# Order of the first pair's nine products in the up projection of a fused two-layer encoder kernel

## The reference, cut to what matters

```python
def conv_ffn(x, g, w_up, conv_w, conv_b, w_down, conv_buf):
    up = rmsnorm(x, g) @ w_up                      # (T, 1024) @ (1024, 2 * 2816)
    full = jnp.concatenate([conv_buf, up], axis=1)
    c = conv_b + full[:, 0:T] * conv_w[0]
    for j in range(1, CONV_W):
        c = c + full[:, j:j + T] * conv_w[j]
    y = (gelu(c[..., :D_FF]) * c[..., D_FF:]) @ w_down
```

## Time and profile before

| | |
|---|---|
| median of 3 runs | 2530.64 us |
| the profiled execution, its own time | 2534.01 us |
| its span | 2532.2 us (1.8 us lie around it) |
| TensorE busy | 2455.9 us, 97% of the span |
| VectorE, ScalarE, GpSimd busy | 1655.4, 1052.1, 579.3 us |
| TensorE in the chain that ended last | 85% of the span |
| mean granted TensorE clock | 0.986 of full speed |

### The profile page before, as it was taken

One profiled execution on the slowest core, in us unless ns is written; L12 is line 12 of the kernel. 1 busy time (PEld: TensorE's weight loads), 2 busy tenths in 40 slices (PEclk: granted clock), 3 DMA queues, 4 the chain that ended last, 5 costly groups with the idle time before them and its releaser, 6 DMA issues.

```text
span 2532.2 us, 41744 instructions
## 1 busy us (share of the span) xinstructions
PE 2455.9 (97%) x16499; PEld 2384.9 (94%) x16499; DVE 1655.4 (65%) x2825; ACT 1052.1 (42%) x1905; POOL 579.3 (23%) x526
## 2 busy tenths in 40 slices
PE   8999989889999999999999999998999999999998
PEld 8999878889999999999999998887999999999997
DVE  3116789788888887464611267888888888864554
ACT  6324544443333333343433355444433333333443
POOL 0001234542222221010110113337322222200111
PEclk9999999999999999999999999998999999999999
DMA  4442322212222223555525333211222222245554
GB/s 149 131 131 93 110 80 65 63 49 70 77 77 74 64 76 110 190 170 162 192 70 154 108 112 104 69 48 53 69 76 77 77 68 70 77 157 175 180 166 157
DMA packets 234903, 265.88 MB, mean 105 GB/s; under 512 B 15287, under 2 KB 207573, under 8 KB 232533
## 3 DMA queue, kind: packets, MB, share of 16 engines
q1 hardware_dynamic: 234708, 263.21, 32.8%
HBM read 213.06 MB, written 50.11 MB: 104 GB/s over the span
## 4 chain that ended last, share of the span: by engine, by line
PE 85%; DVE 8%; issue 3%; POOL 2%; ACT 1%; DMA 1%; SPq 0%; DVEq 0%; POOLq 0%; ACTq 0%
PE bank L317 26%; PE bank L319 25%; PE bank L318 25%; PE bank L1041 2%; DVE prob L1936 1%; PE bank L968 1%; DVE hc L1997 1%; PE bank L1026 1%; PE bank L1010 1%; PE bank L1051 0%; DVE mixA L1964 0%; PE bank L990 0%; PE bank L921 0%; POOL wN L1682 0%; PE bank L1020 0%
## 5 line engine op out<-in xcount | busy, mean ns | idle before, releaser
L317 PE MATMUL bank<-actH,wb 128*128 128x384 f32 (+1 forms) x1552 | 509.6, 328 | 0.3
L318 PE MATMUL bank<-actL,wb 128*128 128x384 f32 (+1 forms) x1552 | 505.4, 326 | 0.0
L319 PE MATMUL bank<-actH,wb 128*128 128x384 f32 (+1 forms) x1552 | 504.7, 325 | 0.0
L317 PE MATMUL bank<-wzH,actH 128*128 128x256 f32 (+3 forms) x1296 | 370.1, 286 | 5.0 <-DVE wzL L1811 4.1
L319 PE MATMUL bank<-wzH,actL 128*128 128x256 f32 (+3 forms) x1296 | 365.3, 282 | 0.0
L318 PE MATMUL bank<-wzL,actH 128*128 128x256 f32 (+3 forms) x1296 | 364.9, 282 | 0.0
L317 PEld LDWEIGHTS bank<-actH,wb 128*128 128x128 f32 x1552 | 292.8, 189 | 5.5 <-issue 4.7
L318 PEld LDWEIGHTS bank<-actL,wb 128*128 128x128 f32 x1552 | 293.4, 189 | 0.5
L319 PEld LDWEIGHTS bank<-actH,wb 128*128 128x128 f32 x1552 | 293.6, 189 | 0.0
L317 PEld LDWEIGHTS bank<-wzH,actH 128*128 128x128 f32 (+1 forms) x1296 | 237.4, 183 | 7.6 <-issue 5.9
L317 PE MATMUL bank<-tH,wb 128*128 128x384 f32 x704 | 237.3, 337 | 1.2 <-ACT vn L1632 1.2
(11 more groups left out here) (289 smaller groups left out, 5229.4 us busy)
## 6 DMA issues: line engine op xcount, KB each, us to landing
raw<-in_w_up SPq DMA_DIRECT2D x88, 512.0 KB, 4.6
raw<-in_w_down SPq DMA_DIRECT2D x88, 512.0 KB, 3.6
g_scratch<-cv SPq DMA_DIRECT2D x44, 545.0 KB, 3.2
rawz<-in_w_in SPq DMA_DIRECT2D x22, 1024.0 KB, 5.5
zb<-z_scratch SPq DMA_DIRECT2D x16, 1156.0 KB, 5.4
tHf<-g_scratch SPq DMA_DIRECT2D x88, 192.0 KB, 3.6
z_scratch<-zst SPq DMA_DIRECT2D x128, 128.0 KB, 1.8
raw<-in_w_out SPq DMA_DIRECT2D x128, 128.0 KB, 2.9
```

The lines of the kernel that those rows point to most:

```text
L317: pe.matmul(out, aH, bH, start=first, stop=False)
L318: pe.matmul(out, aH, bL, start=False, stop=False)
L319: return pe.matmul(out, aL, bH, start=False, stop=last)
```

## The change

Three engines get another order, for the first pair of each layer alone. The work is the same.

TensorE: P1, P2, E, F, P5, `norm_sum`, P6, P7, `norm_row`, P3, P4. The waits before E and F move with them, and P2 gets the wait for `b_l` (low parts) of count 8.

ScalarE: `square_last(5)`, `(6)` and `(7)` follow each other, then come the `norm_high` of the last chunk with `first_copy(0)` between them, then all four `sum_high`, then all four `sums_high`. Before, the `sum_high` and `sums_high` stood between the squares and the `norm_high`.

VectorE: the last three `add_out`, with `weights_low(0, 1)` between them, then all eight `norm_low`, then the low parts of the sums (`tL` 0, three `sum_low`, `tL` 1, `tL` 2). Before, the latter came first and between. From `take` 1 on the order is the old one; the counts waited for follow the new numbering (`product_at`).

GpSimd: the order is kept. The weight sums of the second pair wait for P5, P6, P7 and P3 of the first by their new numbers.

```diff
--- before.py
+++ after.py
@@ -473,6 +473,11 @@
 
             return (l * (NF + NF + NF // 2) + p + 1) * 16
 
+        def product_at(p, name):
+
+            return (("P1", "P2", "E", "F", "P5", "P6", "P7", "P3", "P4") if p == 0 else
+                    ("P1", "P5", "P2", "P6", "P7", "E", "P3", "P4", "F")).index(name) + 1
+
         def step_mm(l, i, m=KT - 1):
 
             c, f = i // NF, i % NF
@@ -1132,37 +1137,54 @@
                         else:
                             pe.wait_ge(take_r, 9 * q - 9 + count)
 
+                    def plain_gate():
+                        if first:
+                            pe.wait_ge(act_l, act_at(n, 2) + KT)
+                        free(6, 24)
+                        plain(4, t[:, 0], t[:, 1])
+
+                    def plain_value():
+                        pe.wait_ge(w_l, weight_at(l, p, 1))
+                        free(9, 24)
+                        plain(5, t[:, 2], t[:, 3])
+
                     pe.wait_ge(w_l, weight_at(l, p, 0))
                     low_parts(4)
                     free(1, 21)
                     quarter(0, t[:, 0, LO], t[:, 1, LO], actH[:, LO, C0], actL[:, LO, C0])
 
+                    if first:
+                        low_parts(8)
+                        free(2, 22)
+                        quarter(1, t[:, 0, HI], t[:, 1, HI], actH[:, HI, C0], actL[:, HI, C0])
+                        plain_gate()
+                        plain_value()
+
                     pe.wait_ge(s_l, 4 * q + 1)
                     low_parts(12)
                     free(7, 23)
                     quarter(2, Sx[:, 0, 0], Sx[:, 0, 1], tH[:, 0], tL[:, 0])
 
-                    free(2, 22)
-                    quarter(1, t[:, 0, HI], t[:, 1, HI], actH[:, HI, C0], actL[:, HI, C0])
+                    if first:
+                        pe.wait_ge(x_r, l * N_X + 16)
+                        norm_sum(pe, n, 2)
+                    else:
+                        free(2, 22)
+                        quarter(1, t[:, 0, HI], t[:, 1, HI], actH[:, HI, C0], actL[:, HI, C0])
 
                     pe.wait_ge(s_l, 4 * q + 3)
                     low_parts(16)
                     pe.wait_ge(copy_r, q + 1)
                     quarter(0, Sx[:, 1, 0], Sx[:, 1, 1], tH[:, 1], tL[:, 1])
-                    if first:
-                        pe.wait_ge(x_r, l * N_X + 16)
-                        norm_sum(pe, n, 2)
 
                     low_parts(20)
                     free(8, 24)
                     quarter(3, Sx[:, 2, 0], Sx[:, 2, 1], tH[:, 2], tL[:, 2])
 
                     if first:
-                        pe.wait_ge(act_l, act_at(n, 2) + KT)
-                    free(6, 24)
-                    plain(4, t[:, 0], t[:, 1])
-                    if first:
                         norm_row(pe, n, 2)
+                    else:
+                        plain_gate()
 
                     pe.wait_ge(s_l, 4 * q + 4)
                     low_parts(24)
@@ -1175,8 +1197,7 @@
                     quarter(3, t[:, 2, HI], t[:, 3, HI], actH[:, LO, C1], actL[:, LO, C1])
 
                     if not first:
-                        pe.wait_ge(take_r, 9 * q)
-                    plain(5, t[:, 2], t[:, 3])
+                        plain_value()
 
                 for p in range(NF):
                     pair(p)
@@ -1577,24 +1598,19 @@
                 for k in range(4):
                     act.wait_ge(t_r, l * 12 + k + 1)
                     act.activation(tH[:, 0, k], xw[:, 4 + k], ACT.Copy).then_inc(b_h, 1)
-                for s in range(3):
-                    sum_high(0, s)
                 square_last(5)
-                sum_high(0, 3)
-                sums_high(0)
                 square_last(6)
-                sums_high(1)
                 square_last(7)
                 act.wait_ge(bank_free, F0 + WU + KT)
                 norm_high(act, n, 2, 0)
                 norm_high(act, n, 2, 1)
                 first_copy(0)
-                sums_high(2)
-                norm_high(act, n, 2, 2)
-                norm_high(act, n, 2, 3)
-                sums_high(3)
-                for m in range(4, KT):
+                for m in range(2, KT):
                     norm_high(act, n, 2, m)
+                for s in range(4):
+                    sum_high(0, s)
+                for k in range(4):
+                    sums_high(k)
 
                 for p in range(NF):
                     ahead = p + 1 < NF
@@ -1753,7 +1769,7 @@
                         pool.wait_ge(raw_in[0], raw_at(l, p))
                         pool.wait_ge(raw_in[1], raw_at(l, p))
                     if p:
-                        pool.wait_ge(mm, tile_mm(l, p - 1, (2, 4, 5, 7)[s]))
+                        pool.wait_ge(mm, tile_mm(l, p - 1, product_at(p - 1, ("P5", "P6", "P7", "P3")[s])))
                     else:
                         pool.wait_ge(mm, l * MMS + WU + (5, 5, 6, 6)[s])
                     if s in (1, 3):
@@ -2103,37 +2119,29 @@
                 for k in range(4):
                     part_low(actL[:, 4 + k, C0], xw[:, k], actH[:, 4 + k, C0], 4 + k + 1)
                 add_out(4)
+                add_out(5)
+                weights_low(0, 1)
+                add_out(6)
+                add_out(7)
+                dve.memset(upb1[:, 0:PAD], 0.0).then_inc(x_r, 1)
+                dve.memset(upb2[:, 0:PAD], 0.0).then_inc(x_r, 1)
+                for m in range(KT):
+                    norm_low(dve, n, 2, m)
                 for k in range(4):
                     part_low(tL[:, 0, k], xw[:, 4 + k], tH[:, 0, k], 16 + k + 1)
                 sum_low(0, 0)
-                add_out(5)
-                weights_low(0, 1)
                 sum_low(0, 2)
-                add_out(6)
                 sum_low(0, 1)
-                add_out(7)
-                dve.memset(upb1[:, 0:PAD], 0.0).then_inc(x_r, 1)
-                dve.memset(upb2[:, 0:PAD], 0.0).then_inc(x_r, 1)
-
-                def second_low(k):
+                for k in range(4):
                     dve.wait_ge(t_r, l * 12 + 4 + 2 * k + 2)
                     part_low(tL[:, 1, k], tLf[:, 1, k], tH[:, 1, k], 20 + 2 * k + 1)
-
-                second_low(0)
-                second_low(1)
-                norm_low(dve, n, 2, 0)
-                norm_low(dve, n, 2, 1)
-                second_low(2)
-                second_low(3)
                 for k in range(4):
                     part_low(tL[:, 2, k], tLf[:, 2, k], tH[:, 2, k], 12 + k + 1)
-                for m in range(2, KT):
-                    norm_low(dve, n, 2, m)
 
                 def take(p, i, out, b, other):
 
                     q = l * NF + p
-                    dve.wait_ge(mm, tile_mm(l, p, TAKEN[i]))
+                    dve.wait_ge(mm, tile_mm(l, p, product_at(p, TAKEN[i])))
                     dve.tensor_tensor(out, bank[b][:, 0:out.shape[1]], other, ALU.mult if i in (6, 9) else ALU.add).then_inc(take_r, 1)
 
                 U0, U1, U2 = slice(PAD, PAD + 384), slice(PAD + 384, PAD + 768), slice(PAD + 768, PAD + TC)
@@ -2308,7 +2316,7 @@
 INIT = 10
 
 
-TAKEN = {1: 4, 2: 3, 3: 2, 4: 5, 5: 5, 6: 6, 7: 7, 8: 8, 9: 9}
+TAKEN = {1: "P6", 2: "P2", 3: "P5", 4: "P7", 5: "P7", 6: "E", 7: "P3", 8: "P4", 9: "F"}
 
 
 _INS = ["x_prompt", "x_sample", "cache_k", "cache_v", "state_C", "state_n", "state_m", "cache_conv", "attn_norm",
```

## The result

The changed kernel takes 2553.5 us in place of 2530.0: the ratio is 1.0094, 95% interval 1.0081 to 1.0107. It is **slower by 23.6 us**. The forecast was 2549.6, in a range of 2540 to 2559.

A forecast was written before the change was run, and what follows sets the result against it. TensorE, busy for 97% of the span, was taken as the bound, so its idle and slow time count. The first take 8.3 us later per layer plus one clock fall, 2 x 8.3 + 2.4 = 19.0, on 2530.6 gives 2549.6; range 2540 to 2559.

The forecast's parts named there:

- The gate of E: TensorE's start of E, waiting for all eight `norm_low`: forecast at 511.7, between 509.3 and 514.3, after idling 13.1 us.
- E and F at half clock: E and F restart at half clock after the wait: 7.1 + 2.4 = 9.5 us, to 521.2.
- The first take: VectorE's first take behind P6: forecast at 526.7 in place of 518.42, 8.3 us later.
- From the first take to the second pair's P6: Stretch behind P6 of the first pair, set by VectorE's chain: forecast unchanged at 24.95 us, P6 at 551.7.
- The clock at the second pair: TensorE's 3.6 us wait before the second pair's P6: clock falls in one of the two layers, 2.4 us.
- Behind P6 VectorE's chain has the same links: From the first take to the second pair's P6: the chain starts 8.3 us late and keeps its length, 24.95 us.
- the rival on the tail: The 24.95 us behind P6 are waits for E and F, so TensorE sets the pace: 2523.4 us; chance 0.03.
- `norm_sum` one product earlier: TensorE issues `norm_sum` before P6: claimed to give nothing, as `norm_mean` stands behind take 1, which waits for P6.
- The full lock: VectorE's `norm_low` and GpSimd take strict turns of 1.5 us: E at 514.1, 2554.4 us in all; chance 0.15.
- The 0.9 us per `norm_low`: Price of each VectorE `norm_low` while GpSimd works, from 1.81 us for two; 0.48 without.

The follow-up runs named there:

- squares_late: The changed kernel with ScalarE's squares 6 and 7 moved behind `norm_high` and `sum_high`: ratio 1.0020, +5.1 us against the kernel before.
- mean_first: The changed kernel with `norm_mean` alone moved ahead of take 1 on VectorE: ratio 1.0064, +16.2 us against the kernel before.
- before_diag_early: The kernel before, with `norm_sum` ahead of P6, `norm_mean` ahead of the last six `norm_low`, `norm_diag` right behind take 3: ratio 0.9993, -1.8 us.

## Why the prediction was right

*The gate of E.* Right. Forecast 511.7, measured 511.61, and from P1, which came 0.7 us earlier in that run, 18.1 in place of 17.6. Its reasons hold one by one: add 5 ended at 503.4 for 504.0, square 7 ran at 503.45 for 504.1, the `norm_high` ended at 507.9 for 508.8, and the eight `norm_low` took 7.15 for 6.6. squares_late shows the cause. That the two starts of E agree to 0.1 us is partly luck: P1 came 0.7 us early, and the `norm_low` took 0.6 longer than I had them.

*E and F at half clock.* 9.76 and 9.2 us for 9.5. P5 found its parts ready, as forecast.

*The first take* came 8.9 and 8.6 us later than before when both are counted from P1 (33.1 for 24.3 in the first layer), for 8.3. P5, `norm_sum` and P6 took what was said.

*From the first take to the second pair's P6:* 25.4 for 24.95, another 0.5 us. In the trace VectorE's `sum_low(1, 3)` takes 1.75 us beside a sum of GpSimd, where it took 0.69 before.

*The clock at the second pair* is **the term that was mis-sized**. I counted one fall of 2.4 us in the two layers. It fell in both, in waits of 4.7 and 3.6 us, and cost 2.8 and 2.4, 5.2 in all. This is 2.8 of the 4.6 us by which the forecast fell short. The other 1.8 us are the P6 of the second pair, 9.4 and 9.1 us later, counted from P1, for 8.3.

*"Behind P6 VectorE's chain has the same links"* held as a sum, and **its reason did not hold**. I took 24.95 us as VectorE's own work with GpSimd's power of 3.12 us in it, and in the rival on the tail I asked only for waits for E and F. mean_first shows 3 us in it that are neither: the power of 0.86 us lasts 3.12 beside VectorE's reads, and `norm_diag` is stretched by GpSimd's sums. I said that `norm_sum` one product earlier gives nothing as long as `norm_mean` stands behind take 1. That was right, and moving `norm_mean` was worth 6.5 us in the tail of the two layers.

*The full lock* as a rival: E would have come at 514.1, and it came at 511.6. But the turns that it describes are there, and **what I held against it was misread**. The 0.9 us per `norm_low` is a mean of 0.59 and 1.30: the first of the two started late in an instruction of GpSimd, the second beside a whole one.

```profile
507.85 0.59 DVE L432 SCALAR_TENSOR_TENSOR actL<-xT,gains,actH 128x322 fp32r<-128x322 f32 x1 [0.64 <-ACT actH L426]
...
508.36 1.30 DVE L432 SCALAR_TENSOR_TENSOR actL<-xT,gains,actH 128x322 fp32r<-128x322 f32 x1
```

In the changed kernel five `norm_low` pass while GpSimd makes five instructions (the last four are shown), and the other three, behind it, take 0.47 each:

```profile
505.34 1.12 POOL L365 TENSOR_TENSOR acc<-acc,sqn 128x322 f32<-128x322 f32 x1
...
506.42 1.11 POOL L1798 TENSOR_TENSOR tLf<-actF,xw 128x384 f32<-128x384 f32 x1
...
507.61 1.12 POOL L1800 TENSOR_TENSOR actF<-xw,tLf 128x384 f32<-128x384 f32 x1
...
508.70 1.12 POOL L365 TENSOR_TENSOR acc<-acc,sqn 128x322 f32<-128x322 f32 x1
```

That is one for one, five and three, as this rival counted them. What it had wrong is the price of a turn: 1.14 us on average, and not the sum of 1.02 and 0.48. The forecast's 0.9 was too low for a turn too, which was hidden in part: GpSimd's loop ended 0.5 us earlier, counted from P1, than I had it, so that fewer `norm_low` ran beside it. The Trainium skill (SBUF — State Buffer, "Who interferes with whom") calls the shared port an exclusive lock. The turns agree with it; that a turn is shorter than the two lengths together shows that some 0.3 us of them overlap here.

## What to carry to other kernels

When work is moved ahead, follow its inputs through every queue to the instruction that waits for another engine: here two squares of half a microsecond stood on ScalarE ahead of the inputs of 7 us of products, and cost 16 of 24 us. Count the clock as well as the wait: the waits of 3.1 to 4.7 us before the second pair's P6 cost TensorE another 1.3 to 2.8 us behind them, and those of 1.9 us and less nothing. And before a chain is called one engine's own work, compare the lengths of its instructions with the same ones elsewhere in the trace, one by one: a mean over some that ran beside another engine and some that ran alone is the price of neither.

## What the runs showed of the hardware

VectorE's instructions with two inputs in SBUF and GpSimd's take turns: in the changed kernel each of five `norm_low` ends 0.35 us behind the end of an instruction of GpSimd (505.73 for 505.38, then 506.81 for 506.46, and so on to 510.16 for 509.81). So VectorE's pace is that of GpSimd, 1.14 us for 0.47 alone. GpSimd's own, 0.86 to 1.0 us alone, take some 1.12 there. Beside sums of 512 columns it is dearer still: from 0.41 to 1.48 us (`norm_diag`), from 0.49 to some 1.6 (a single `part_low` or `norm_low`). The takes, with one input in PSUM, took 0.53 each in all kernels.

It can also be GpSimd that waits, and then VectorE loses nothing. Its power on 3 columns takes 0.86 us alone, 1.11 beside `norm_low`, and 3.12 beside a `sum_low` and four `part_low`, which took 1.95 us there as alone. A sum of 512 columns, which takes as little as 1.26 us elsewhere, took 4.90 in before_diag_early, while VectorE's two `weights_low` beside it kept their 1.2 us each:

```profile
527.42 4.90 POOL L1763 TENSOR_TENSOR Sf<-raw,Sf 128x512 f32<-128x512 f32 x1 [5.46 <-PE bank L319]
```
